# Attention heads taken in groups of 512 columns, with GpSimd subtracting the maxima of class heads, and differential attention in the tile order 3, 0, 2, 1

## Chip, cores and metric

One core of one Trainium2 chip. The metric is the device time of one launch in microseconds; of the kernel before three runs are shown.

## The reference, cut to what matters

The model has two blocks of two layers, all in float32, for 512 tokens of width 1024. The change touches four kinds of attention.

```python
# first block, in both layers: 8 plain heads over 2 key heads, width 64
sc = einsum('bqgrd,bkgd->bgrqk', qi, k) * scale
o = einsum('bgrqk,bkgd->bqgrd', softmax(sc), v)
# and three dilated groups of 4 heads: window 128 at step 1, 512 at 4, 2048 at 16
sc = where(valid, einsum('bqhd,bqkhd->bhqk', qi, kg) * scale + bias, -inf)
lse = logsumexp(sc); o = einsum('bhqk,bqkhd->bqhd', exp(sc - lse), vg)
# the three groups are merged by softmax over their lse
# second block, layer 0: differential attention, 8 heads, causal
p = softmax(where(dist >= 0, q @ k + bias, -inf))      # two maps m = 0, 1
attn = p[:, :, 0] - lam_full * p[:, :, 1]; out = attn @ v
# second block, layer 1: causal window of 128, 8 heads over 2 key heads, a sink a head
p = softmax(concatenate([q @ k + bias, sink]))[..., :-1]; out = p @ v
```

## The kernel before, in words

Tokens lie on the 128 partitions in NT = 4 tiles. The kernel is a chain of stages; `stage` (L63) ends each with a barrier of all engines. In a stage each engine runs its own program in order, and they meet at semaphores. `Link` (L50) makes DVE wait for its own last instruction.

**`attention` (L1564)** serves the first block's attention (called at L2362 from `first_layer`, once for each of the two layers, in a loop) and the window attention (called at L3580 from `odd_mixer`). Its work is a list of units, one unit being one head and one query tile. `global_units` (L2383) makes 32 units with 512 keys, `dilated_units` (L2394) 48: for each tile and head one "band" unit with 256 keys (step 1) and two "class" units with 128 keys (tokens are sorted by class, so that the wider steps become dense blocks of 128). `odd_mixer` makes 32 units of 256 keys, 128 in the first tile.

For unit i, PE multiplies queries and keys into one of four PSUM banks (L1610, 64 of the 128 rows; heads with even number lie on partitions 0 to 63, odd ones on 64 to 127). DVE finds the row maximum: L1658 for plain heads, negated in one step; with a bias L1665 adds it, writes the sum to `sc` and takes the maximum, and L1668 negates. In the window attention L1667 takes the sink into the maximum. ACT takes the exp with the negated maximum as its bias and the sum as its accumulator output (L1642; L1641 for the sink). PE transposes the result in blocks of 128 (L1617), DVE copies them out of PSUM (L1675), PE multiplies with V (L1627 through `chain`, L84) and DVE scales with the reciprocal of the sum, or, for dilated heads, only copies (L1682 to L1688). PE's order in step i is: scores of i+2, transposes of i-1, products of i-2; DVE's: maxima of i, copy of i-2, result of i-3. 12 warm-up products (`warm_up`, L98) stand at the start. SyncE meanwhile loads the bias tables, writes 11.8 MB of zeros to `slots_x` and brings V of the band heads into order through DRAM (`order_v0`, L1540); the first dilated unit waits for all of that.

`branches` (L1692) merges the dilated results on DVE (L1864 to L1887) beside PE's gates; `in_projection` (L1362) writes V.

**`diff_attention` (L3113)** has 32 units: 8 heads, in each the tiles t = 0, 1, 2, 3 with 128 (t + 1) keys. The two maps of a head lie on partitions 0 to 63 and 64 to 127. For each unit:

```python
link(V.tensor_tensor_reduce(sc.., ps.., b, 1.0, 2 * NEG, ALU.add, ALU.max, mx..))   # L3216, m = 0, 1
V.tensor_scalar(nm.., mx.., -1.0, None, ALU.mult)                                 # L3218
link(V.reciprocal(l, l)); link(V.tensor_tensor(l[:, 1:2], l[:, 1:2], nlam[:], ALU.mult))
link(V.tensor_scalar(p0, p0, l[:, 0:1], None, ALU.mult))                          # L3226
V.scalar_tensor_tensor(p0, p1, l[:, 1:2], p0, ALU.mult, ALU.add)                  # L3227
```

DVE runs the maxima of unit i, then combines the maps of unit i-1. ACT runs the exps of i (L3178), the copy of the transposes of i-1 (L3186) and the output copy of i-2 (L3191); half-way it rounds the next weights (`round_ahead`, L706).

## Time and profile before

| | |
|---|---|
| runs | 3630.17 us median of 3 (3629.97 to 3633.74) |
| the profiled execution's own time | 3633.27 us |
| its span in the profile | 3631.5 us |
| PE, PEld, DVE | busy 3201.4, 2543.0, 2324.2 us |
| ACT, POOL | busy 1214.5, 374.9 us |
| mean granted clock of PE | 0.919 |

PE is TensorE's matrix products, PEld its weight loads, DVE VectorE, ACT ScalarE, POOL GpSimd, SP SyncE. Matrix products are pipelined and their ends are modelled, so their durations overlap; starts are safer to subtract. The granted clock is a share of full speed. In a group, "idle before" is the time that the engine stood still ahead of those instructions, with what ended it.

### The profile page before, as it was taken

What the parts mean: (1) busy time and instruction counts of PE and PEld (TensorE: products, weight loads), DVE (VectorE), ACT (ScalarE), POOL (GpSimd) and SP (SyncE); (2) the same over time, 40 slices, a digit from 0 to 9 for tenths busy, and PEclk for the clock granted to TensorE, in tenths of its full rate; (3) what the DMA queues carried; (4) which work ended last, traced back from release to release, by engine and by line L of the source; (5) the groups of instructions that cost most, each with busy time, mean ns of one, the idle gap of its engine ahead of it and who ended that gap; (6) DMA issues with size and microseconds to landing.
All of it is one profiled execution on the core that took longest, in us unless ns stands there. A gap on an engine that the chain in (4) does not pass through costs nothing. (4 is left out here: it accounts for less than half of the span.)

```text
span 3631.5 us, 40689 instructions
## 1 busy us (share of the span) xinstructions
PE 3201.4 (88%) x14731; PEld 2543.0 (70%) x14731; DVE 2324.2 (64%) x3761; ACT 1214.5 (33%) x1713; POOL 374.9 (10%) x136
## 2 busy tenths in 40 slices
PE   4999996996799896899499789889999898989999
PEld 3777775774676685777377578757887687658887
DVE  6766666897676657599733747667664575564445
ACT  2323224664323322476322624431111222231111
POOL 0000001000000000100000000304444000004443
PEclk9999996998799998799789799989999899869999
DMA  7751724997655353599652034024442452103222
GB/s 256 238 171 61 242 101 141 360 405 278 216 171 168 135 185 99 193 401 403 243 170 100 1 102 139 27 82 133 148 144 74 136 182 79 53 24 105 92 92 81
DMA packets 285304, 583.89 MB, mean 161 GB/s; under 512 B 21561, under 2 KB 129537, under 8 KB 278076
## 3 DMA queue, kind: packets, MB, share of 16 engines
q1 hardware_dynamic: 272744, 537.83, 42.8%
q10 hardware_dynamic: 7764, 26.85, 1.8%
q0 software_dynamic: 4608, 16.78, 1.2%
q8 instruction: 109, 1.79, 0.2%
q14 instruction: 79, 0.65, 0.1%
HBM read 529.44 MB, written 78.70 MB: 167 GB/s over the span
## 5 line engine op out<-in xcount | busy, mean ns | idle before, releaser
L132 ACT CAST w_hi<-ring 128x2048 fp32r<-128x2048 f32 (+2 forms) x166 | 308.1, 1859 | 1213.5 <-PE ps L283 1030.9
L283 PE MATMUL ps<-hT_hi,w_hi 128*128 128x512 f32 (+1 forms) x1256 | 501.1, 399 | 25.2 <-DVEq L1117 12.6
L283 PE MATMUL ps<-hT_lo,w_hi 128*128 128x512 f32 (+1 forms) x1256 | 498.6, 397 | 0.0
L139 POOL TENSOR_TENSOR w_lo<-ring,w_hi 128x2048 fp32r<-128x2048 f32 x64 | 307.2, 4802 | 935.9 <-ACTq L2854 552.7
L144 DVE TENSOR_TENSOR w_lo<-ring,w_hi 128x2048 fp32r<-128x2048 f32 (+3 forms) x112 | 245.4, 2195 | 233.5 <-ACT w_hi L132 233.2
L283 PE MATMUL ps<-hT_hi,w_lo 128*128 128x512 f32 (+1 forms) x1256 | 305.2, 395 | 10.2 <-DVE w_lo L144 10.2
L283 PEld LDWEIGHTS ps<-hT_hi,w_hi 128*128 128x128 f32 (+1 forms) x1256 | 238.6, 190 | 85.6 <-DVEq L1117 14.2
L283 PEld LDWEIGHTS ps<-hT_hi,w_lo 128*128 128x128 f32 (+1 forms) x1256 | 235.7, 188 | 67.3 <-DVE w_lo L144 12.2
L1054 DVE SCALAR_TENSOR_TENSOR piece_sums<-pieces,cond,piece_sums 128x512 f32<-128x512 f32 x294 | 220.7, 751 | 90.4 <-DMA pieces<-in_w_ada_dram 57.8
L283 PEld LDWEIGHTS ps<-hT_lo,w_hi 128*128 128x128 f32 (+1 forms) x1256 | 238.6, 190 | 55.5
L283 PE MATMUL ps<-w_hi,hT_hi 128*128 128x512 f32 (+1 forms) x672 | 259.9, 389 | 1.0 <-ACT w_hi L132 1.0
L283 PE MATMUL ps<-w_hi,hT_lo 128*128 128x512 f32 (+1 forms) x672 | 259.0, 387 | 0.0
L283 PE MATMUL ps<-w_hi,hid_hi 128*128 128x512 f32 x448 | 174.4, 389 | 0.0
L283 PE MATMUL ps<-w_hi,hid_lo 128*128 128x512 f32 x448 | 174.4, 389 | 0.0
L2919 DVE TENSOR_TENSOR hid_exact<-hid_exact 128x512 f32<-128x512 f32 x64 | 162.0, 2531 | 4.0 <-DVE hid_exact L2916 0.6
L283 PE MATMUL ps<-w_lo,hT_hi 128*128 128x512 f32 (+1 forms) x672 | 158.2, 387 | 0.0
L2058 POOL DMA_INDIRECT slots_x<-ring,rows_r x16 | 21.5, 1345 | 1212.9 <-DVE rows_r L2271 1208.6
L283 PEld LDWEIGHTS ps<-w_hi,hT_hi 128*128 128x128 f32 x672 | 126.4, 188 | 28.6 <-issue 1.8
L283 PEld LDWEIGHTS ps<-w_hi,hT_lo 128*128 128x128 f32 x672 | 126.4, 188 | 26.8
L102 PE MATMUL ps<-ident_sb 128*128 128x128 f32 x664 | 99.7, 324 | 49.6 <-PEq L72 49.6
L283 PEld LDWEIGHTS ps<-w_lo,hT_hi 128*128 128x128 f32 x672 | 124.2, 188 | 27.3 <-DVE w_lo L144 0.3
L102 PEld LDWEIGHTS ps<-ident_sb 128*128 128x128 f32 x664 | 97.6, 238 | 52.9 <-issue 52.9
(594 smaller groups left out, 6258.3 us busy)
## 6 DMA issues: line engine op xcount, KB each, us to landing
ring<-in_mlp_w_dram SPq DMA_DIRECT2D x64, 1024.0 KB, 5.2
pieces<-in_w_ada_dram SPq DMA_DIRECT2D x96, 512.0 KB, 6.0
ring<-in_w_in_dram SPq DMA_DIRECT2D x36, 1024.0 KB, 7.0
pieces<-in_mod_w_dram SPq DMA_DIRECT2D x72, 512.0 KB, 5.3
raw_sep<-in_w_exp_gate_dram SPq DMA_DIRECT2D x50, 512.0 KB
raw_sep<-in_w_exp_up_dram SPq DMA_DIRECT2D x50, 512.0 KB
raw_sep<-in_w_exp_down_dram SPq DMA_DIRECT2D x24, 1024.0 KB
ring<-in_e_w_in_dram SPq DMA_DIRECT2D x24, 1024.0 KB, 5.5
```

What stands on the lines that cost most here:

```text
L102: pe.matmul(k.ps[:, bank, 0:P], k.ident[:], k.ident[:], start=True, stop=True)
L132: self.k.nc.scalar.copy(self.k.parts[0][:, i, 0:words], self.k.ring[:, i, 0:words]).then_inc(self.high, 1)
L139: self.k.nc.gpsimd.tensor_tensor(self.k.parts[1][:, i, 0:words], self.k.ring[:, i, 0:words], self.k.parts[0][:, i, 0:words].bitcast(F32), ...
L144: self.k.nc.vector.tensor_tensor(self.k.parts[1][:, i, 0:words], self.k.ring[:, i, 0:words], self.k.parts[0][:, i, 0:words].bitcast(F32), ...
L283: mm = pe.matmul(out, a if weight_left else b, b if weight_left else a, start=first and part == 0 and q == ks[0] and o == 0, stop=last and ...
L1054: ins = V.scalar_tensor_tensor(acc, slot[:, q, :], f, acc, ALU.mult, ALU.add)
L2058: nc.gpsimd.indirect_dma_start(k.slots_x, bass.IndirectOffsetOnAxis(rows[:, i, t:t + 1], 0), xn[:, t, :], None).then_inc(scattered, 16)
L2919: link(V.tensor_tensor(e, e, e, ALU.mult))
```

## The change

The units become groups that fill one PSUM bank of 512 columns: one plain head, four class heads, two band heads, and two window heads (four in the first tile). The two groups of a pair lie on opposite halves of the partitions, and PE takes their scores head by head in turn, for two groups ahead. For dilated and window groups one DVE instruction adds the bias and one takes all maxima, negated; for class groups GpSimd subtracts the maxima and ACT takes one exp of 512 columns. V of the dilated heads gets a 65th column of ones, so that the product brings the sum and the exp needs no accumulator. ACT makes the copies of the transposes for every second plain group and for all others. `sc` has three buffers for two, `pr` three for four. The window attention has 28 warm-up products. In the differential attention the maxima come out negated, the scale of p0 moves into the output copy, and the tiles go in the order 3, 0, 2, 1.

The diff, cut to its core (not shown: the layout of the bias tables, the `[:, :, 0:HD]` in the copies of `in_projection`, `order_v0` with 260-wide rows, the views in `branches`):

```diff
@@ in_projection
+            link(V.memset(T["vc"][:, :, :, HD:HD + 1], 1.0))
+            link(V.memset(v0c[:, :, :, HD:HD + 1], 1.0))
@@ attention(k, groups, loads=(), space=None, late=(), ahead=None, warm=12)
-        pr, sc, pT = idle[:, 0:4], idle[:, 4:6], idle[:, 6:8]
+        pr, sc, pT = idle[:, 0:3], idle[:, 3:6], idle[:, 6:8]
+        width = lambda i: 512 // heads(i)
+        of_class = [u["kind"] == "dilated" and len(u["heads"]) == 4 for u in groups]
+        by_act = [u["kind"] != "global" or i % 2 == 1 for i, u in enumerate(groups)]
@@ tensor
+            def scores(a):
+                b = a + 1
+                if b >= 4:
+                    pe.wait_ge(exp_done, b - 3)
+                for h in range(heads(a)):
+                    last_a, last_b = score(a, h), score(b, h)
+                last_a.then_inc(s_ready, 1)
+                last_b.then_inc(s_ready, 1)
+            warm_up(k, pe, 4, warm)
             for i in range(-2, N + 2):
+                if i % 2 == 0 and i + 2 < N:
+                    scores(i + 2)
                 if 1 <= i <= N:
...
-                    for j in range(W(v) // P):
+                    for j in range(4):
...
+                    for h, (_q, _k, vs) in enumerate(groups[v]["heads"]):
+                        n, w = vs[0].shape[-1], width(v)
+                        mm = chain(pe, k.ps[:, 4 + v % 2, h * n:(h + 1) * n], lambda j: pT[:, v % 2, h * w + j * P:h * w + (j + 1) * P],
+                                   lambda j: vs[j], range(len(vs)))
@@ scalar
+            def soften(i):
...
+                if u["kind"] == "global":
+                    last = nc.scalar.activation(p, k.ps[:, bank[i % 4], :], ACT.Exp, bias=nm(i), accum_out=ls[:, i % 4, 0:1])
+                elif of_class[i]:
+                    last = nc.scalar.activation(p, sc[:, i % 3], ACT.Exp)
+                else:
+                    w = width(i)
+                    if u["kind"] == "window":
+                        nc.scalar.activation(es[:, i % 4, 0:heads(i)], es[:, i % 4, 0:heads(i)], ACT.Exp)
+                    for h in range(heads(i)):
...
+                        last = nc.scalar.activation(p[:, at], sc[:, i % 3, at], ACT.Exp, bias=nm(i)[:, h:h + 1], accum_out=total)
+            for i in range(N + 1):
+                if i < N:
+                    soften(i)
+                v = i - 1
+                if v >= 0 and by_act[v]:
+                    act.wait_ge(t_ready, v + 1)
+                    if v >= 2:
+                        act.wait_ge(o_ready, v - 1)
+                    nc.scalar.copy(pT[:, v % 2], k.ps[:, 2 + v % 2, :]).then_inc(t_act, 1)
@@ gpsimd
+            for i in range(N):
+                if of_class[i]:
+                    pool.wait_ge(max_done, i + 1)
+                    x = per_head(sc[:, i % 3], i)
+                    nc.gpsimd.tensor_tensor(x, x, bcast(nm(i), 2, width(i)), ALU.add).then_inc(less_done, 1)
@@ vector
+            def maxima(i):
...
+                if u["kind"] == "global":
+                    V.tensor_reduce(nm(i), s, AX, ALU.max, negate=True).then_inc(max_done, 1)
+                    return
...
+                if i >= 3:
+                    dve.wait_ge(exp_done, i - 2)
+                x = per_head(sc[:, i % 3], i)
+                link(V.tensor_tensor(x, per_head(s, i), u["bias"], ALU.add))
+                ins = V.tensor_reduce(nm(i), x, AX, ALU.max, negate=True)
+                if u["kind"] == "window":
+                    link(ins)
+                    link(V.tensor_tensor(nm(i), nm(i), u["less_sink"], ALU.min))
+                    ins = V.tensor_tensor(es[:, i % 4, 0:heads(i)], nm(i), u["less_sink"], ALU.subtract)
+                ins.then_inc(max_done, 1)
...
+            for i in range(-1, N + 2):
+                if i + 1 < N:
+                    maxima(i + 1)
+                v = i - 1
+                if 0 <= v < N and not by_act[v]:
...
+                if i >= 2:
+                    result(i - 2)
@@ diff_attention
-        units = [(h, t) for h in range(8) for t in range(NT)]
+        units = [(h, t) for h in range(8) for t in (3, 0, 2, 1)]
@@ scalar
-                        last = nc.scalar.activation(pr[:, i % 2, m, 0:W(i)], sc[:, i % 2, m, 0:W(i)], ACT.Exp,
+                        last = nc.scalar.activation(pr[:, i % 2, m, 0:W(i)], sc[:, i % 2, m, 0:W(i)], ACT.Exp, scale=-1.0,
...
-                    nc.scalar.copy(y[:, t, h * P:(h + 1) * P], k.ps[:, 6 + u % 2, 0:P]).then_inc(o_out, 1)
+                    nc.scalar.activation(y[:, t, h * P:(h + 1) * P], k.ps[:, 6 + u % 2, 0:P], ACT.Copy, scale=inv[:, u % 4, 0:1]).then_inc(o_out, 1)
@@ vector
-                        link(V.tensor_tensor_reduce(sc[:, i % 2, m, 0:W(i)], k.ps[:, 2 * (i % 2) + m, 0:W(i)], b, 1.0, 2 * NEG,
-                                                    ALU.add, ALU.max, mx[:, i % 2, m:m + 1]))
-                    V.tensor_scalar(nm[:, i % 2, :], mx[:, i % 2, :], -1.0, None, ALU.mult).then_inc(max_done, 1)
+                        V.tensor_tensor_reduce(sc[:, i % 2, m, 0:W(i)], k.ps[:, 2 * (i % 2) + m, 0:W(i)], b, -1.0, -2 * NEG,
+                                               ALU.add, ALU.min, nm[:, i % 2, m:m + 1]).then_inc(max_done, 1)
...
+                    if u >= 4:
+                        dve.wait_ge(o_out, u - 3)
+                    link(V.reciprocal(inv[:, u % 4, :], l))
+                    link(V.scalar_tensor_tensor(r, l[:, 0:1], inv[:, u % 4, 1:2], nlam[:], ALU.mult, ALU.mult))
...
-                    link(V.tensor_scalar(p0, p0, l[:, 0:1], None, ALU.mult))
-                    V.scalar_tensor_tensor(p0, p1, l[:, 1:2], p0, ALU.mult, ALU.add).then_inc(p_ready, 1)
+                    V.scalar_tensor_tensor(p0, p1, r, p0, ALU.mult, ALU.add).then_inc(p_ready, 1)
@@ retention_projection
+                    link(V.tensor_scalar(sink[:], sink[:], -1.0, None, ALU.mult))
@@ odd_mixer
+            attention(k, groups, warm=28, space=space, late=moves, ahead=[(ring(i), wo[:, KD:KD + 4, 512 * i:512 * (i + 1)]) for i in range(2)])
```

## Rows read from the trace of the kernel before

**Rows 1.** Busy time by stage: us, busy us (xinstructions) by engine, clock, DMA, GB/s.
```profile
213.60:292.70 79.10, 79.04 (x445) 52.95 (x446) 53.04 (x120) 26.20 (x65) 0.00 (x0) 1.00 0.60 193
292.70:345.80 53.10, 52.23 (x316) 39.73 (x316) 44.09 (x249) 25.44 (x96) 0.00 (x0) 1.00 0.01 1
1987.00:2087.50 100.50, 74.83 (x382) 51.48 (x381) 74.17 (x297) 61.35 (x196) 0.00 (x0) 0.80 0.07 23
3131.00:3201.30 70.30, 66.70 (x257) 48.13 (x257) 49.22 (x257) 25.59 (x97) 0.00 (x0) 0.62 0.18 68
```

**Rows 2.** Timeline, plain heads: start us, us, engine, line, operation, tiles, count.
```profile
287.68 1.12 PE L1610 MATMUL ps<-kaT,qaT 64*128 64x512 f32 x2
...
288.73 0.66 PE L1617 MATMUL ps<-ident_sb,ring 128*128 128x128 f32 x4
...
289.12 0.97 PEld L84 LDWEIGHTS ps<-kva,ring 128*128 128x128 f32 x8
...
290.15 0.29 PEld L1610 LDWEIGHTS ps<-k0T,q0T 64*128 64x128 f32 x2
```

**Rows 3.** Timeline of PE, differential attention: both maps' scores of one tile.
```profile
1993.30 1.13 PE L3148 MATMUL ps<-kT,qT 64*128 64x512 f32 x4
...
2008.14 0.49 PE L3148 MATMUL ps<-kT,qT 64*128 64x128 f32 x4
```

**Rows 4.** Timeline of PE, dilated heads: two scores and the transposes after them.
```profile
335.71 0.49 PE L1610 MATMUL ps<-kcT,qcT 64*128 64x128 f32 x2
336.13 0.33 PE L1617 MATMUL ps<-ident_sb,ring 128*128 128x128 f32 x1
...
336.56 0.70 PE L1610 MATMUL ps<-k0T,q0T 64*128 64x256 f32 x2
337.19 0.44 PE L1617 MATMUL ps<-ident_sb,ring 128*128 128x128 f32 x2
```

**Rows 5.** Groups of instructions by shape, GpSimd: xcount, busy us, mean ns, idle before.
```profile
L2998 POOL TENSOR_TENSOR Xdec<-Xdt,dte 128x256 f32<-128x256 f32 x16 | 9.8, 612 | 536.7 <-DVE Xdt L3074 531.7 <-PE ps L3068 5.0
...
L3001 POOL TENSOR_TENSOR xh<-xh,par 128x1024 f32<-128x1024 f32 x4 | 7.8, 1946 | 0.0
```

**Rows 6.** Groups by shape, whole span, DVE and ACT.
```profile
L1642 ACT ACTIVATE ring<-ps,nm 128x512 f32<-128x512 f32 x64 | 44.0, 687 | 104.7 <-DVE nm L1658 104.4
...
L1658 DVE TENSOR_REDUCE nm<-ps 128x1 f32<-128x512 f32 x64 | 43.6, 682 | 10.8 <-PE ps L1610 10.8
...
L1642 ACT ACTIVATE ring<-ring,nm 128x128 f32<-128x128 f32 x64 | 25.7, 402 | 21.1 <-DVE nm L1668 20.8
...
L1675 DVE COPY ring<-ps 128x256 f32<-128x256 f32 x32 | 13.6, 425 | 10.0 <-PE ps L1617 9.8
```

**Rows 7.** Timeline of SyncE's queue in the attention of the first layer.
```profile
265.26 1.56 SPq L1594 DMA_DIRECT2D v<-scratch  x3
```

**Rows 8.** Timeline of PE, window attention: warm-up, then one unit.
```profile
3131.19 4.38 PE L102 MATMUL ps<-ident_sb 128*128 128x128 f32 x24 [3.54 <-PEq L72]
...
3153.45 1.22 PE L1610 MATMUL ps<-skT,sqT 64*128 64x256 f32 x2
3154.60 0.69 PE L1617 MATMUL ps<-ident_sb,attention_space 128*128 128x128 f32 x2
3155.08 0.95 PE L84 MATMUL ps<-skv,attention_space 128*128 128x64 f32 x4
3155.96 1.22 PE L1610 MATMUL ps<-skT,sqT 64*128 64x256 f32 x2
```

**Rows 9.** Timeline of DVE, differential attention: maxima at the start of two heads.
```profile
2010.33 0.28 DVE L3216 CUSTOM_DVE_ANT_0 attention_space<-ps,bias 128x128 f32<-128x128 f32 x1
...
2021.28 0.28 DVE L3216 CUSTOM_DVE_ANT_0 attention_space<-ps,bias 128x128 f32<-128x128 f32 x1
```

**Rows 10.** Groups by shape, differential attention: the scaling of p0, the output copy.
```profile
L3226 DVE TENSOR_SCALAR attention_space<-attention_space,dls 128x512 f32<-128x512 f32 x8 | 3.9, 486 | 0.3
...
L3191 ACT COPY y<-ps 128x128 f32<-128x128 f32 x32 | 8.6, 267 | 11.4 <-PE ps L84 11.2
```

More of the change, by code:

```diff
@@ L1561, in qkd_dst, with attention @@
     return dst, p, mul
-def attention(k, units, loads=(), space=None, late=(), ahead=None):
+def attention(k, groups, loads=(), space=None, late=(), ahead=None, warm=12):
     nc = k.nc
@@ new lines, in result @@
+            def result(v):
+                u, n = groups[v], heads(v)
+                dve.wait_ge(o_ready, v + 1)
+                d = u["heads"][0][2][0].shape[-1]
+                po = k.ps[:, 4 + v % 2, 0:n * d]
+                if u["kind"] == "dilated":
+                    V.tensor_copy(u["out"], po.rearrange("p (h d) -> p h d", h=n)).then_inc(o_out, 1)
+                    return
+                l = ls[:, v % 4, 0:n]
+                if u["kind"] == "window":
+                    link(V.tensor_tensor(l, l, es[:, v % 4, 0:n], ALU.add))
+                link(V.reciprocal(l, l))
+                if n == 1:
+                    V.tensor_scalar(u["out"], po, l, None, ALU.mult).then_inc(o_out, 1)
+                else:
+                    V.tensor_tensor(u["out"], po.rearrange("p (h d) -> p h d", h=n), bcast(l, 2, d), ALU.mult).then_inc(o_out, 1)
@@ L2380, in first_layer, with global_groups @@
                mod=(next_sums[:, 0:2 * D], A["b_ada"][DEPTH - 1][0:2 * D], 16, k.mod, (8,), None))
-def global_units(T):
-    units = []
-    for h in range(A_HEADS):
-        p0, g = 64 * (h % 2), h // 4
+def global_groups(T):
+    groups = []
+    for pair in range(A_HEADS // 2):
         for t in range(NT):
-            units.append(dict(q=T["qaT"][p0:p0 + 64, h // 2, t * P:(t + 1) * P], k=T["kaT"][p0:p0 + 64, g, :],
-                              v=[T["kva"][:, j, 128 + 64 * g:192 + 64 * g] for j in range(NT)],
-                              out=T["oa"][:, t, h * HD:(h + 1) * HD]))
-    return units
@@ new lines, in global_groups, with dilated_groups @@
+    return groups
+def dilated_groups(T, band, cls):
+    groups = []
+    for t in range(NT):
+        for odd in range(2):
+            rows, heads = slice(64 * odd, 64 * odd + 64), []
+            for g in range(2):
+                for half in range(2):
+                    q, kk = (T[n][rows, 2 * g + half, t * P:(t + 1) * P] for n in ("qcT", "kcT"))
+                    heads.append((q, kk, [T["vc"][:, t, BG * g + 2 * half + odd, :]]))
+            u = T["U12"][:, 2 * t + odd].rearrange("p g h d -> p (g h) d")
+            groups.append(dict(kind="dilated", heads=heads, bias=cls[:, odd], out=u[:, :, 0:HD + 1], nm=u[:, :, HD + 1]))
+        for odd in range(2):
+            rows, heads = slice(64 * odd, 64 * odd + 64), []
+            for half in range(2):
+                heads.append((T["q0T"][rows, half, t * P:(t + 1) * P], T["k0T"][rows, half, t * P:t * P + 256],
+                              [T["v0"][:, t + j, 2 * half + odd, :] for j in range(2)]))
+            u = T["U0"][:, 2 * t + odd]
+            groups.append(dict(kind="dilated", heads=heads, bias=band[:, 0 if t == 0 else 2 if t == NT - 1 else 1, odd],
+                               out=u[:, :, 0:HD + 1], nm=u[:, :, HD + 1]))
+    return groups
@@ L3579, in odd_mixer @@
             ring = lambda i: k.ring[:, i, :].rearrange("p (k n) -> p k n", k=4)
-            attention(k, units, space=space, late=moves, ahead=[(ring(i), wo[:, KD:KD + 4, 512 * i:512 * (i + 1)]) for i in range(2)])
+            attention(k, groups, warm=28, space=space, late=moves, ahead=[(ring(i), wo[:, KD:KD + 4, 512 * i:512 * (i + 1)]) for i in range(2)])
             hT = pair_of(nc, h, "hT", [P, KD, S], side="right")
```

226 lines of the change are left out of this document (100 added, 126 removed).

## The prediction

> **What bounds the kernel now.** I first took the busy table of four stretches [rows 1]: the plain heads of the first block's attention (214 to 293 us; the second layer repeats it at 1097), its dilated heads (293 to 346), the differential attention (1987 to 2087) and the window attention (3131 to 3201). The reader is to see that PE is busy for nearly the whole of the first two at a granted clock of 1.00, that no engine is full in the third (clock 0.80), and that the fourth has PE full at 0.62. The two layers' attention fills 265 us, the other two 166 us; the rest of the 3631 us is hardly touched.
>
> The timeline says what PE does there. One plain head and tile takes 2.47 us, from its score at 287.68 to the next at 290.15 [rows 2]: score 1.05 (to 288.73), four transposes 0.39 (to 289.12), eight products with V 1.03. PE is the bound. In the differential attention, where the two maps' scores lie in different halves of the array's rows, both 512-wide scores take 1.13 us and both 128-wide ones 0.49 [rows 3]; a single head's 128-wide score lasts as long, 0.49, and the next transpose starts 0.42 after it [rows 4]. So a pair in opposite halves costs what one costs. The change makes such pairs everywhere.
>
> **Plain heads (32 units a layer).** Heads 2k and 2k+1 go through the same tile as a pair. PE per pair: scores 1.06 (the 1.05 of rows 2, with 0.01 for the second as 1.13 stands to 1.12), transposes 2 x 0.39, products 2 x 1.03: 3.90, or 1.95 a unit against 2.47. Do the others keep up? DVE is busy 53.0 us for 32 units now [rows 1], 1.66 each, and gives every second copy (0.68, as the 512-wide maximum on PSUM in rows 6) to ACT: 1.32 of 1.95. ACT's 26.2 us are 0.82 each, with half a copy 1.17. I followed one pair round, PE's cycle from 0 to 3.9: its first products end at 2.5, DVE then moves that result, takes the next maximum (to 3.6), copies the transposes (to 4.4), moves the second result, takes the second maximum (to 5.5); ACT, behind its own copy (to 6.1), has the second exp by 7.0, and the scores that wait for it come at 7.8. So PE stays the bound, with 0.8 to spare: 32 x 0.52 = 16.6 us, less 1 for filling the pipeline, **-16 a layer**. From below it is 0 if pairs don't overlap; from above 16.6. The last loads that the dilated heads wait for start at 265.26 and are issued by 266.8 [rows 7]; the first dilated maximum moves from 292.7 to about 277, so 10 us of cover are left.
>
> **Dilated heads (48 units become 16 groups of 512 columns).** PE for two class groups: four pairs of 128-wide scores at 0.42 [rows 4], 1.68; transposes 0.78; products 2.06: 4.52. For two band groups: two pairs of 256 at 0.63, 1.26 + 0.78 + 2.06 = 4.10. Mean 2.16 a group. Now the loop through the others: DVE adds the bias and takes four maxima in one instruction; each is 512 wide, so each 0.68 as the plain maximum, 1.41 for both with gaps. It moves a result out in 0.43 [rows 6]. GpSimd's subtraction of 512 columns is not in the trace: 256 take 0.61 and 1024 with a broadcast 1.95 [rows 5], so about 1.05; at the least 0.61, at the most 1.95. Exp 0.69 at most. From the end of one group's products: result 0.43, maxima 1.41, result 0.43, maxima 1.41, GpSimd 1.05, exp 0.69, eight handovers of 0.05, then scores 1.68, transposes 0.39 and products 1.03 on PE: 8.9 us for four groups, 2.23 a group. So the chain of DVE and GpSimd binds by a hair, and PE waits 3%. The new waits in it: ACT's exp for GpSimd, with the copy of the group before queued behind it, and PE's paired scores for the exp of two pairs ago, with the next transposes behind them. 16 x 2.23 = 35.7, and 3 for the last group's tail: 38.7 against 53.0 now (292.7 to 345.7), **-14 a layer**. Bounds: GpSimd at 0.61 leaves PE as the bound (-15.5); at 1.95 four groups take 9.8 and it is -11.
>
> Here the Trainium skill speaks against the change. "GPSIMD Engine Reference", section 8, says that GpSimd shares its SBUF interfaces with DVE, and that DVE's instructions with two SBUF inputs or in a two-port mode get in its way. No row here shows the two side by side in such a stage; by that rule the subtraction moves towards the 1.95 bound.
>
> **Window attention (32 units become 14 groups).** The stage goes at two rates. From 3151.3 PE runs at half clock: scores of 256 take 1.15 (3153.45 to 3154.60), two transposes 0.48, four products 0.88 [rows 8]; a unit 2.51, two units 5.0. A new group, two heads, takes 1.15 (its pair's scores shared by two) + 0.96 + 1.76 = 3.87 there. At full clock a group's DVE work binds: 1.41 as above and six small ones. DVE's 49.2 us for 32 units [rows 1] are 1.54 each, of which two 256-wide ones take 0.85 and five small ones 0.69, so 0.14 each or 0.2 with gaps: 2.5 us to 2.6. I take 6 groups at 2.5 and 8 at 3.87, 46, and 4 for start and tail: 50 against 65.8 now (3135.5 to 3201.3). Before it stand 28 warm-up products for 12: those 24 instructions took 4.38 us [rows 8], 0.18 each, and at the higher clock at the least half of it: 32 more cost 2.9 to 5.8, I take 5. **-11**; bounds -2 (all at half, long warm-up) and -23 (all at full).
>
> **Differential attention (32 units).** A head of four units takes 10.95 us between its first maxima [rows 9]. DVE loses the negation of the maxima (some 0.08 of time a unit) and the scaling of p0, 0.49 for the widest and less in step for the others, 1.7 a head with gaps [rows 10]; the scale moves into ACT's copy of the output, where a pointer operand costs between nothing and 0.13 more on 0.27 (a whole 128-wide exp with its pointer takes 0.40) [rows 6, 10]. So 1.9 us of DVE work a head goes. It sits in a loop (maxima, exp, combine, transpose, copy) in which PE waits longest for DVE, so most of it counts: I take 1.6. The new order puts a 512-wide tile next to a 128-wide one, so that a long maxima stands beside a short combine; I give it nothing of its own, since the first head starts later by 0.8 and the last unit's tail is shorter by about 1. 8 x 1.6 = **-13**; bounds 0 and -23 (DVE without any idle time, 2.9 a head). The added wait for the output copy of unit u-4 holds up the combine on DVE and with it PE's transposes; that copy is three units old by then, so it is free.
>
> **Small edits.** Two memsets with a link at the start of the projection, while DVE waits for weights; copies to 65-wide rows of the same 512 columns; one more short add for the merged heads, beside PE's gates; one scaling of the sinks. +1 in all.
>
> **Sum:** -32 - 28 - 11 - 13 + 1 = -83. The profiled execution took 3633.3 us, so 3550; it stands 3.1 above the median of 3630.2, so **3548 us**.
>
> **Rivals.**
> (a) PE's clock falls in the dilated stage. For: the chain is as long as PE's own work, so PE waits a little in each group, and in the window stage, with PE busy 95%, the rows fall to half rate and stay there for 50 us [rows 1, 8]. Against: the dilated stage of before, in which DVE is as close to full, holds 1.00 to its tail. Price, from the half-rate rows: four groups take 3.1 and 2.3 for scores (1.15 stands to 0.63 as 1.83), 3.8 for transposes, 7.0 for products, so a group 4.07 against 2.23, 59 us over both layers: 3607. Chance 0.14.
> (b) The slower side: it falls in the plain stage too. A unit would take (1.93 + 1.92 + 3.52) / 2 = 3.7 against 1.95, 112 us more over both layers, 171 with the dilated: 3719; from half of both stages at half clock on, the kernel is slower than before. For: transposes become a larger share of PE's work. Against: PE has work in every microsecond there. Chance 0.05. The Trainium skill, "TensorE: Matmul & The Clock Gate", Part 4, says that transposes don't count as activity for the clock gate; by that rule this rival is likelier, but no row of before shows it, since the dilated stage with its transposes holds full clock.
> (c) The pairs don't overlap where heads change from product to product, since only two maps of one head are seen to. Plain heads +34 (32 pairs of 1.06), dilated +24 (2.94 for four groups), window +4: 3610. Chance 0.06.
> (d) It goes better: the window stage stays at full clock (-12), the differential attention loses nearly all its idle time (-10), GpSimd is quicker (-3): 3523. Chance 0.20.
> My forecast, 3530 to 3570, has 0.50; what lies in between the cases, 0.05.
>
> **Numbers.** The range reaches over (d) and most mixtures with (a): 3515 to 3600. 0.2% (7 us) is about what a measurement of this kernel can tell from no change. Faster 0.93, same 0.02, slower 0.05.
>
> **What would show it.** Right: a plain pair in 3.9 us, with two 512-wide scores in 1.1; dilated groups at 2.2 to 2.3 with GpSimd's instruction near 1.05 us; a head of the differential attention at 9.3; window groups at 2.5, then 3.9. Wrong: scores of a pair one after the other; a granted clock of 0.5 between 217 and 320 us; GpSimd over 1.5 us; PE waiting for DVE in the plain stage; a head that stays near 11 us.

## The result

The changed kernel takes 3510.86 us (median of 4 runs, 3501.62 to 3512.78), the kernel before 3630.42 us beside it: ratio 0.9664, 95% interval 0.9646 to 0.9682, or 120 us less. The prediction had 3548 us and 3515 to 3600: the direction was right, the gain was half as large again as forecast, and the median lies 4 us below the range.

| | before | after |
|---|---|---|
| the profiled execution's own time, us | 3633.27 | 3511.61 |
| its span, us | 3631.5 | 3509.8 |
| PE, PEld, DVE busy, us | 3201.4, 2543.0, 2324.2 | 3075.4, 2487.9, 2230.2 |
| ACT, POOL busy, us | 1214.5, 374.9 | 1220.9, 391.8 |
| mean granted clock of PE | 0.919 | 0.932 |

To find where 122 us of span went, I cut both traces at the same marks: a stage runs from the first DVE or ACT instruction of its function to the first one of the next function. These cuts are used for every experiment below.

| stage, us | before | after | difference | forecast |
|---|---|---|---|---|
| attention, first layer | 133.3 | 97.9 | -35.4 | -30 |
| attention, second layer | 133.3 | 97.9 | -35.4 | -30 |
| differential attention | 139.1 | 120.9 | -18.3 | -13 |
| window attention | 72.0 | 52.3 | -19.7 | -11 |
| projection behind the window | 64.9 | 56.7 | -8.2 | 0 |
| the scan behind the differential attention (`ssd`) | 156.5 | 149.4 | -7.1 | 0 |
| all others, with the MLP behind the scan at +3.7 | | | +2.4 | +1 |

The four stretches of [rows 1] in the kernel after. Columns: start and end in us, its length, busy us (and instructions) of PE, PEld, DVE, ACT and POOL, the granted clock, the share of the DMA engines and GB/s.

```profile
214.30:276.40 62.10, 61.31 (x463) 48.00 (x463) 39.87 (x106) 33.36 (x80) 0.00 (x0) 1.00 0.74 246
276.40:311.00 34.60, 33.35 (x300) 30.14 (x299) 27.43 (x56) 20.14 (x42) 8.38 (x8) 1.00 0.01 1
1911.00:1996.00 85.00, 65.47 (x392) 44.41 (x392) 58.57 (x233) 63.65 (x199) 0.00 (x0) 0.92 0.09 27
3037.00:3087.50 50.50, 40.08 (x289) 35.79 (x289) 30.69 (x99) 25.80 (x93) 0.00 (x0) 0.84 0.25 95
```

PE still fills the first two, at a clock of 1.00. In the other two no engine is full, and the clock rose: 0.80 to 0.92 and 0.62 to 0.84. The plain heads, from the timeline of PE (start, us, engine, line, operation, tiles, count):

```profile
262.05 1.13 PE L1618 MATMUL ps<-kaT,qaT 64*128 64x512 f32 x4
263.11 0.66 PE L1641 MATMUL ps<-ident_sb,ring 128*128 128x128 f32 x4
263.60 1.00 PE L84 MATMUL ps<-kva,ring 128*128 128x64 f32 x8
264.44 0.61 PE L1641 MATMUL ps<-ident_sb,ring 128*128 128x128 f32 x4
264.88 1.00 PE L84 MATMUL ps<-kva,ring 128*128 128x64 f32 x8
265.81 1.13 PE L1618 MATMUL ps<-kaT,qaT 64*128 64x512 f32 x4
```

Both 512-wide scores of a pair take 1.06 us start to start, where the single one of [rows 2] took 1.05, and a pair takes 3.76 us in place of two units of 2.47. One turn of the dilated heads, all engines, with the weight loads left out:

```profile
289.80 1.16 PE L1618 MATMUL ps<-kcT,qcT 64*128 64x128 f32 x16
...
290.90 0.66 PE L1641 MATMUL ps<-ident_sb,ring 128*128 128x128 f32 x4
...
291.39 1.00 PE L84 MATMUL ps<-vc,ring 128*128 128x65 f32 x8
...
292.43 0.43 DVE L1733 COPY U<-ps 128x260 f32<-128x260 f32 x1 [0.97 <-PE ps L84]
...
292.78 0.68 DVE L1719 TENSOR_TENSOR ring<-ps,cls 128x512 f32<-128x512 f32 x1
...
293.50 0.69 DVE L1720 TENSOR_REDUCE U<-ring 128x4 f32<-128x512 f32 x1
293.61 0.73 PEld L1618 LDWEIGHTS ps<-k0T,q0T 64*128 64x128 f32 x8
293.61 1.13 PE L1618 MATMUL ps<-k0T,q0T 64*128 64x256 f32 x8
294.10 0.42 DVE L1733 COPY U<-ps 128x260 f32<-128x260 f32 x1
294.27 1.05 POOL L1699 TENSOR_TENSOR ring<-ring,U 128x512 f32<-128x512 f32 x1 [5.18 <-DVE U L1720]
294.44 0.68 DVE L1719 TENSOR_TENSOR ring<-ps,cls 128x512 f32<-128x512 f32 x1
...
295.92 1.05 POOL L1699 TENSOR_TENSOR ring<-ring,U 128x512 f32<-128x512 f32 x1 [0.61 <-DVE U L1720]
...
297.00 0.63 ACT L1672 ACTIVATE ring<-ring 128x512 f32<-128x512 f32 x1 [0.55 <-POOL ring L1699]
...
297.69 1.16 PE L1618 MATMUL ps<-kcT,qcT 64*128 64x128 f32 x16
```

Read it as the loop of the prediction: the products with V end at 292.4, DVE moves a result, adds the bias and takes the maxima, moves the next result, does it again for the second group, then GpSimd takes its 1.05 us (from 295.92) and ACT its exp (from 297.00), whose end PE's scores at 297.69 follow. The next scores of k0T come 7.88 us after those at 285.73. The differential attention, from DVE's timeline, the first maxima of two heads (a head now begins with its widest tile):

```profile
1936.60 0.69 DVE L3293 CUSTOM_DVE_ANT_0 attention_space<-ps,bias 128x512 f32<-128x512 f32 x1 [0.36 <-PE ps L3225]
...
1944.97 0.69 DVE L3293 CUSTOM_DVE_ANT_0 attention_space<-ps,bias 128x512 f32<-128x512 f32 x1 [0.36 <-PE ps L3225]
```

A head takes 8.37 us, where [rows 9] had 10.95. And the window attention, two groups at full clock, next to [rows 8] at half clock:

```profile
3058.07 1.14 PE L1618 MATMUL ps<-skT,sqT 64*128 64x256 f32 x8
3059.14 0.66 PE L1641 MATMUL ps<-ident_sb,attention_space 128*128 128x128 f32 x4
3059.64 1.00 PE L84 MATMUL ps<-skv,attention_space 128*128 128x64 f32 x8
3060.48 0.60 PE L1641 MATMUL ps<-ident_sb,attention_space 128*128 128x128 f32 x4
3060.92 1.00 PE L84 MATMUL ps<-skv,attention_space 128*128 128x64 f32 x8
3062.62 1.13 PE L1618 MATMUL ps<-skT,sqT 64*128 64x256 f32 x8 [0.70 <-ACT attention_space L1680]
```

### The profile page after: what moved, and what is told of

Same layout as the page of the kernel before. It is cut to its first block and busy times, and to the rows that moved or that the text cites. A ratio compares the mean times of both kernels' runs of the same rounds, so it can differ in the third digit from the quotient of the medians.

```text
span 3509.8 us, 39676 instructions
## 1 busy us (share of the span) xinstructions
PE 3075.4 (88%) x14763; PEld 2487.9 (71%) x14763; DVE 2230.2 (64%) x3130; ACT 1220.9 (35%) x1629; POOL 391.8 (11%) x152
## 5 line engine op out<-in xcount | busy, mean ns | idle before, releaser
L3015 DVE TENSOR_TENSOR y<-y,ps 128x512 f32<-128x512 f32 x48 | 33.0, 688 | 157.1 <-PE ps L283 155.8
```

The lines of the kernel that those rows point to most:

```text
L3015: link(V.tensor_tensor(yv, yv, k.ps[:, 4 * b + t, :], ALU.add))
```

## The experiments

| run | us (median) | ratio to before, 95% interval |
|---|---|---|
| p1_first_block | 3561.25 | 0.9808 (0.9777 to 0.9840) |
| p2_differential | 3616.43 | 0.9949 (0.9933 to 0.9965) |
| p3_window | 3610.04 | 0.9942 (0.9925 to 0.9959) |
| p4_warm_up_alone | 3632.15 | 0.9995 (0.9981 to 1.0010) |
| q1_order_undone | 3508.95 | 0.9665 (0.9645 to 0.9685) |
| q2_order_alone | 3628.18 | 0.9983 (0.9970 to 0.9996) |
| q3_short_warm_up | 3517.59 | 0.9691 (0.9670 to 0.9711) |
| q4_subtraction_on_DVE | 3515.44 | 0.9676 (0.9653 to 0.9699) |
| r1_GpSimd_twice | 3531.27 | 0.9722 (0.9695 to 0.9749) |
| r2_unpaired_scores | 3580.27 | 0.9861 (0.9835 to 0.9887) |
| r3_round_on_GpSimd | 3511.07 | 0.9671 (0.9646 to 0.9695) |
| r4_scaling_back_on_DVE | 3521.24 | 0.9692 (0.9658 to 0.9725) |
| s1_window_unpaired | 3528.16 | one run |
| s2_window_order_1230 | 3510.56 | 0.9663 (0.9639 to 0.9687) |
| s3_all_three | 3506.23 | 0.9644 (0.9625 to 0.9663) |

On the chips of these runs the kernel before ranged from 3621 to 3643 us, wider than in the first comparison; differences of a few us are therefore read from the stages of the profiled executions, not from the medians.

### The parts, each alone

**p1_first_block**: the new attention for the two layers of the first block; the differential and window attention as before.

```diff
-def diff_attention(...):   # after
+def diff_attention(...):   # before
-            attention(k, groups, warm=28, space=space, ...)
+            unit_attention(k, units, space=space, ...)
```

> The new groups in the attention of the first block's two layers alone; the differential and the window attention as before. Theory: all of the gain that the trace shows in these two stages is their own: 133.3 us become 97.9 each, so -71, and the 3.7 us between the two layers belong to them too (the merging of the heads): 3555 us. Rival: what lies outside the touched stages (-12 us in all) is a change of the granted clock that comes with any shift in time; then the stages give -71 as well, but the rest moves by several us either way, and stages that are not touched here show another clock than in the kernel before.

The two stages took 99.5 and 99.4 us, the kernel 70.5 us less: the gain of these stages is their own. The 1.6 us over the 97.9 of the changed kernel is a stretch of 3.4 us at half clock that the records show in the first 5 us of the stage, in its warm-up: those 24 instructions took 4.55 us here and 2.92 in the first layer of the changed kernel. It comes in some executions of either kernel and not in others (134.9 against 133.3 in the kernel before). Two other stages differ with the same code: `ssd` took 156.3 us here and the projection behind the window 64.9, where the changed kernel has 149.4 and 56.7.

**p2_differential**: the new `diff_attention` in the kernel before.

```diff
-def diff_attention(...):   # before
+def diff_attention(...):   # after
```

> The new differential attention alone, the rest as before. Theory: a head takes 8.4 us in place of 10.95 whatever stands ahead of it, the stage gives -19: 3611 us. Rival: part of those 19 us came from the granted clock, which was 0.92 in this stage after the change and 0.80 before, because the stage began at another time; then heads take 9 us or more here, and the kernel 3616 or more.

A head took 8.37 us, exactly as in the changed kernel, although the stage began 73 us later; the stage took 117.7 us against 139.1. So the gain doesn't hang on when the stage begins, and the rival's usual heads of 9 us or more didn't come. The kernel's median, 3616, is the rival's all the same: in the profile `ssd` and the projection behind the window stand at 157.6 and 65.2 us. How much of the head's gain comes through the clock is seen below.

**p3_window**: the groups and 28 warm-up products in the window attention of the kernel before.

```diff
-            attention(k, units, space=space, ...)
+            group_attention(k, groups, warm=28, space=space, ...)
```

> The new groups and the long warm-up in the window attention alone, the rest as before. Theory: groups keep the array busy enough for the full clock, 2.3 us a group, the stage gives -20, and the projection after it starts at full clock and gives some 7 more: about 3604 us. Rival: it was luck of the clock; then groups at half clock take 3.9 us, the stage gives -11 or less and nothing follows: 3619 us or more.

The stage took 54.4 us and the projection behind it 62.6, where the changed kernel has 52.3 and 56.7. The stage's gain comes with the groups and their pairs (s1 parts the two); what follows it varies (below).

**p4_warm_up_alone**: 28 warm-up products for 12 in the window attention of the kernel before.

```diff
-            attention(k, units, space=space, ...)
+            attention(k, units, warm=28, space=space, ...)
```

> The kernel before with 28 warm-up products in place of 12 in the window attention, its 32 single units unchanged. Theory: the warm-up only costs, 3 to 5 us, and the units fall to half clock as before: 3633 to 3635 us. Rival: the longer warm-up is what lifts the clock; then a unit of 2.5 us takes about 1.5 for most of the stage, and the kernel is 10 to 20 us faster.

The stage took 77.0 us, against 72.0 to 75.0 in the profiles with 12 products and single units, and from 20 us after its start to its end, 57 us, its records show half clock (52 in the kernel before). The warm-up alone brings nothing and costs 2 to 5 us.

The three parts sum to -70.5 - 15.3 - 21.7 = -107.5 us, the whole is -119.6. The touched stages alone, in the profiles, gave 67.8 + 21.5 + 17.6 = 106.9 us one by one and 108.8 together. So the difference of 12 us lies in stages that none of them touches: `ssd` takes 149.2 to 157.6 us over the profiles of the study and the projection behind the window 56.7 to 65.2, each with one and the same code, by how many stretches at half clock fall into them. In the profile of before both stood near their long end (156.5, 64.9), in that of after near their short one.

### The scores of a pair

**r2_unpaired_scores**: each group's scores by themselves.

```diff
-                if i % 2 == 0 and i + 2 < N:
+                if i + 2 < N:
                     scores(i + 2)
...
-                b = a + 1
-                if b >= 4:
-                    pe.wait_ge(exp_done, b - 3)
+                if a >= 4:
+                    pe.wait_ge(exp_done, a - 3)
                 for h in range(heads(a)):
-                    last_a, last_b = score(a, h), score(b, h)
-                last_a.then_inc(s_ready, 1)
-                last_b.then_inc(s_ready, 1)
+                    last = score(a, h)
+                last.then_inc(s_ready, 1)
```

> The changed kernel with each group's scores issued by themselves, as before the change, one group ahead of the other; everything else stays grouped. Leaves the pairs of opposite halves out. Theory: the pairs are the gain of the plain heads and a good part of that of the dilated ones. A plain unit is 2.4 us again, +16 us a layer; two class groups' scores take 3.4 in place of 1.16 and two band groups' 2.5 in place of 1.13, so +3.6 for four groups or +14 a layer; the window +8: about 3580 us in all. Rival: grouping and the split of the copies between DVE and ACT are the gain, PE had been waiting more than its records say; then less than +10 a layer.

A layer's attention took 123.9 us (+26), the window stage 72.9 (+20.6), the kernel 3580 us, as expected in sum but not in its terms. PE's timeline, plain heads first, then the dilated ones:

```profile
249.70 1.12 PE L1618 MATMUL ps<-kaT,qaT 64*128 64x512 f32 x2
250.75 0.66 PE L1639 MATMUL ps<-ident_sb,ring 128*128 128x128 f32 x4
251.25 1.00 PE L84 MATMUL ps<-kva,ring 128*128 128x64 f32 x8
252.18 1.12 PE L1618 MATMUL ps<-kaT,qaT 64*128 64x512 f32 x2
...
301.88 1.16 PE L1618 MATMUL ps<-kcT,qcT 64*128 64x128 f32 x8
302.97 0.66 PE L1639 MATMUL ps<-ident_sb,ring 128*128 128x128 f32 x4
...
304.40 1.13 PE L1618 MATMUL ps<-k0T,q0T 64*128 64x256 f32 x4
305.45 0.66 PE L1639 MATMUL ps<-ident_sb,ring 128*128 128x128 f32 x4
```

A plain unit is back at 2.48 us, 1.2 more a pair; from the first maximum to the dilated heads' a layer took 74.6 us for 58.0. But four class scores of one group, one after the other, take 1.09 us, so 0.27 each, where I had put 1.7, and two band scores 1.05, where I had put 1.25. The 0.42 of [rows 4] is a score that stands alone in front of a transpose; in a run of scores it costs less. Four dilated groups took 10.0 us for 7.88, +2.1 and not +3.6, and the window stage made up for it with +20.6 where I had +8.

### What sets the dilated stage

**q4_subtraction_on_DVE**: DVE subtracts the maxima.

```diff
                 ins = V.tensor_reduce(nm(i), x, AX, ALU.max, negate=True)
+                if of_class[i]:
+                    link(ins)
+                    V.tensor_tensor(x, x, bcast(nm(i), 2, width(i)), ALU.add).then_inc(less_done, 1)
+                    return
```

> The changed kernel with the subtraction of the class heads' maxima on DVE in place of GpSimd. Theory: the chain through DVE and GpSimd sets the dilated stage (7.88 us for four groups); it loses two handovers and one 1.05 and gains 0.7 twice, and it delays the result behind it, so 8.2 to 8.6 us, +2 to +3 us a layer. Rival 1: PE sets it, with the chain just under it; then DVE, at 5.6 us of 7.9 now and 7.0 then, still hides, and nothing changes within 1 us. Rival 2: GpSimd's instruction holds up DVE through their shared interfaces; then DVE's own instructions get shorter and the stage is faster than 97.9 us a layer.

Four groups took 8.21 us and a layer 101.5; of its +3.6, 1.6 is the half clock in the warm-up again, and the dilated part took 37.8 us for 35.8. The loop sets the stage, as expected; PE, with 33.35 of 34.6 us busy, comes just under it. The rival of shared interfaces falls: DVE's additions of the bias take 0.68 us here, without GpSimd, as they do beside it.

**r1_GpSimd_twice**: the subtraction is made twice.

```diff
+                    if sum(of_class[:i]):
+                        pool.wait_ge(spare_done, sum(of_class[:i]))
...
+                    nc.gpsimd.tensor_tensor(twice..., x, bcast(nm(i), 2, width(i)), ALU.add).then_inc(spare_done, 1)
                     nc.gpsimd.tensor_tensor(x, x, bcast(nm(i), 2, width(i)), ALU.add).then_inc(less_done, 1)
```

> The changed kernel with GpSimd's subtraction made twice (the first into a spare tile), 16 instructions of 1.05 us more over both layers, nothing else added. Theory: the loop of DVE, GpSimd, ACT and PE sets the dilated stage. Of two neighbouring class groups the second's instruction ends 1.5 us later (0.45 because the first's doubled one runs into it, 1.05 of its own), so four groups take 9.4 in place of 7.9 us: +6 us a layer. Rival: PE's own work sets it; then most of the 1.5 is hidden and a layer gains less than 3 us. If GpSimd also slowed DVE through shared interfaces, the 0.68 us additions of DVE beside it would get longer than they are.

The second layer took 104.5 us (+6.6; its turns 9.6, 10.8 and 9.2 us), as the loop says, the first 111.6 (+13.7, of which 1.6 in the warm-up). Columns as in the table of stretches, dilated heads of the first layer and the end of the second's attention:

```profile
278.00:325.00 47.00, 42.42 (x297) 38.27 (x296) 27.87 (x55) 20.55 (x41) 16.34 (x16) 0.78 0.01 1
1120.00:1160.00 40.00, 35.79 (x305) 31.16 (x305) 27.61 (x60) 19.40 (x42) 12.23 (x12) 0.96 0.04 13
```

With PE waiting 1.3 us or more in each turn (9.2 less 7.9) its clock fell for 20.5 us in the first layer and for 3.4 in the second. So my rival (a), a clock that falls in the dilated stage, didn't happen in any profile with one subtraction, and did with two. DVE's additions stood at 0.68 us again.

### The differential attention

**q1_order_undone** and **q2_order_alone**: the order of the tiles, in the changed kernel and in the one before.

```diff
-        units = [(h, t) for h in range(8) for t in (3, 0, 2, 1)]   # q1; q2 is the reverse
+        units = [(h, t) for h in range(8) for t in range(NT)]
```

> The changed kernel with the differential attention's query tiles in the order 0, 1, 2, 3 again. Theory of the prediction: the order is worth nothing, the gain is DVE's work that was left out; the stage from its start to the projection behind it stays at 121 us, within 2. Rival: the order is worth a good part, since a wide tile's long maxima no longer stand beside a narrow one's short exp; then the stage takes 126 us or more.

> The kernel before, with the order 3, 0, 2, 1 alone. Theory: nothing, the stage stays at 139 us within 2. Rival: it falls to 134 or less, and then the order and the removed instructions share the gain.

**r4_scaling_back_on_DVE**: the scaling of p0 as before, the order and the maxima as after.

```diff
+                    link(V.tensor_scalar(p0, p0, l[:, 0:1], None, ALU.mult))
-                        nc.scalar.activation(y[...], k.ps[...], ACT.Copy, scale=inv[:, u % 4, 0:1]).then_inc(o_out, 1)
+                        nc.scalar.copy(y[...], k.ps[...]).then_inc(o_out, 1)
```

> The changed kernel with the first map's weights scaled by DVE again and ACT's output copy without the scale; the left-out negation and the order stay. The prediction's own price: 1.7 us a head, nearly all of it on the path, 13 us in all: the stage takes 133 to 135 us. Rival: PE's and ACT's work is what is left there, with DVE busy 79%; then it costs 6 us or less, and the rest of the 18 us that the stage gained is from elsewhere (clock, order).

The usual distance between two heads' first maxima, at full clock but for the first row:

| us a head | order 0, 1, 2, 3 | order 3, 0, 2, 1 |
|---|---|---|
| DVE's work as before, with 3.4 to 3.8 us of each head at half clock | 10.85 (before) | |
| DVE's work as before | 10.04 (p1) | 9.76 (q2) |
| negation left out, scaling kept | | 8.96 (r4) |
| both left out | 8.59 (q1) | 8.37 (after) |

In the kernel before every head holds half clock. The 10.04 is in p1's profile, which has the old code here and two heads with 0.4 us of half clock or none; one of them, and beside it the head of [rows 9], in the columns of the stretches:

```profile
1924.09 0.28 DVE L3421 CUSTOM_DVE_ANT_0 attention_space<-ps,bias 128x128 f32<-128x128 f32 x1
...
1934.13 0.28 DVE L3421 CUSTOM_DVE_ANT_0 attention_space<-ps,bias 128x128 f32<-128x128 f32 x1
```

```profile
1924.10:1934.10 10.00, 7.09 (x46) 4.65 (x46) 9.00 (x37) 7.06 (x25) 0.00 (x0) 1.00 0.01 2
```

```profile
2010.30:2021.30 11.00, 8.56 (x46) 5.76 (x46) 9.17 (x38) 7.19 (x25) 0.00 (x0) 0.84 0.00 0
```

At full clock the order is worth 0.3 us a head with DVE's old work and 0.2 with the new, and the left-out work 1.45 in the old order and 1.4 in the new: they add up, to 1.7. The other 0.8 of the 2.5 us is half clock, which the usual heads lose with either edit. Over the whole stage the records show 51 us of it before, 38 with the order alone (q2), 27 with the left-out work alone (q1) and 24 after. The stage took 135.1 us in q2 (139.1 before, 138.7 to 141.2 in the other profiles with the old code), between the two cases of its expectation, and 121.1 in q1 (120.9), as the prediction had it. There the 0.2 us a head, 1.8 in all, is lost among other half-clock stretches and another first and last head; the kernel took 3509.

With the scaling kept (r4) the stage took 125.3 us, +4.4 and not the 13 of the prediction's price: 0.6 us a head. The rest of the 1.4, 0.8 (9.76 less 8.96), comes with the negation and the links around it, which stood between the maxima and the exp. Which of the two, instruction or links, was not tried.

**r3_round_on_GpSimd**: the two casts of the next projection's weights go from ACT's row to GpSimd.

```diff
-                if i == N // 2:
-                    round_ahead(k, act, ahead)
+        @block.gpsimd
+        def _(pool):
+            for i in range(2):
+                pool.wait_ge(k.ahead[i], ahead)
+                nc.gpsimd.tensor_copy(k.parts[0][:, i, :], k.ring[:, i, :])
```

> The changed kernel with the rounding of the weights of the next projection, two casts of 2048 columns, 3.7 us together, that stand in ACT's row halfway through the differential attention, given to GpSimd, which is idle there. Theory: the head that holds them takes 13.2 us where others take 8.4, so the stage falls from 121 by 4.5 to 5 us and the kernel to about 3506. Rival 1: GpSimd's casts slow DVE, which is busy 79% there, and half of it comes back. Rival 2: the half clock takes it back (granted 0.92 in this stage).

The fifth head fell from 13.2 to 8.37 us and the stage from 120.9 to 114.8, yet the kernel took 3511 as before: the window stage and its projection took 54.6 and 65.2 in place of 52.3 and 56.7, in code that isn't touched, with 27 and 38 us at half clock in place of 18 and 16. So rival 2 is right in its effect, but not in the stage that it named. GpSimd makes the casts in the first head, as soon as the weights have landed, and not halfway. DVE's and GpSimd's timeline shows one thing more:

```profile
1916.21 2.10 POOL L3275 CAST w_hi<-ring 128x2048 fp32r<-128x2048 f32 x1 [216.97 <-DMA ring<-in_e_w_out_dram]
...
1917.63 0.70 DVE L3306 SCALAR_TENSOR_TENSOR dratio<-dls,dinv,nlam 128x1 f32<-128x1 f32 x1
...
1918.88 1.90 POOL L3275 CAST w_hi<-ring 128x2048 fp32r<-128x2048 f32 x1 [0.56 <-DMA ring<-in_e_w_out_dram]
...
1919.37 0.16 DVE L3305 RECIPROCAL dinv<-dls 128x2 f32<-128x2 f32 x1
...
1919.57 1.22 DVE L3306 SCALAR_TENSOR_TENSOR dratio<-dls,dinv,nlam 128x1 f32<-128x1 f32 x1
1920.82 0.62 DVE L3308 SCALAR_TENSOR_TENSOR attention_space<-attention_space,dratio 128x384 f32<-128x384 f32 x1
```

### The window attention

**q3_short_warm_up**: 12 warm-up products in the changed kernel.

```diff
-            attention(k, groups, warm=28, space=space, ...)
+            attention(k, groups, space=space, ...)
```

> The changed kernel with 12 warm-up products in the window attention in place of 28. Theory: the 32 instructions less save 3 to 5 us and nothing else changes, groups stay at 2.3 us: the stage takes 48 us in place of 52. Rival: the warm-up is what brought the full clock; then groups start at 3.9 us and the stage takes 58 us or more.

51.0 us for the stage, of which its records show 14 at half clock in its middle (6.8 in the changed kernel): groups came to 2.3 us all the same. The warm-up is not what brings the full clock. The kernel took 3517.6 us, more than with 28 products, since the projection behind the window took 65.2 us for 56.7.

**s1_window_unpaired**: the scores as in r2, in this stage alone.

```diff
-                if i % 2 == 0 and i + 2 < N:
+                if i + 2 < N and groups[0]["kind"] == "window":
+                    single(i + 2)
+                elif i % 2 == 0 and i + 2 < N:
                     scores(i + 2)
```

> The changed kernel with the scores issued group by group in the window attention alone; its groups, its long warm-up and the pairs of the first block stay. Theory: it is the pairs that bring the window stage back to full clock, since all profiles with pairs show half clock for 7 to 14 us in it and all without (the single units, and the groups without pairs) for 55 to 65: the stage takes 72 to 75 us in place of 52. Rival: in the kernel without any pairs it stayed at half clock because the stage began at an unlucky time; then it comes back here and the stage takes about 58 us (six pairs of 1.1).

The stage took 72.9 us. Its row, and that of a whole stage of single units in the kernel before:

```profile
3033.00:3106.00 73.00, 68.57 (x297) 58.29 (x298) 31.78 (x100) 27.64 (x95) 0.00 (x0) 0.57 0.17 66
```

```profile
3131.20:3203.10 71.90, 68.50 (x265) 49.89 (x266) 49.41 (x258) 27.31 (x98) 0.00 (x0) 0.62 0.18 67
```

Without pairs the groups and the long warm-up together give this stage nothing (it took 72 to 75 us before); the pairs give all of it. In the ten profiles with pairs the clock falls 10 to 14 us after the stage's start and is back 3.4 to 13.7 us later; in the seven without it falls 13 to 20 us after the start and stays at half to the stage's end, 52 to 62 us, though PE has fewer gaps there (68.6 of 73 us busy against 40.1 of 50.5). In both the first 3 us of the stage are at half clock, and with pairs the last 8 to 11 too. The edit does two things: scores in opposite halves no longer alternate, and PE no longer issues two groups' scores in one go. Which of them brings the clock back, and why, is not shown; that the pairs as a whole do is.

**s2_window_order_1230**: the two groups of four heads last.

```diff
-            for t in range(NT):
+            for t in (1, 2, 3, 0):
```

> The changed kernel with the window attention's query tiles in the order 1, 2, 3, 0, so that the two groups of four heads, in which PE waits 2.8 and 1.1 us for ACT's eight exps, come last. Theory: the half clock that the records show 24.7 us after the stage's start in every profile comes from these waits at its start; it doesn't come, and the stage takes 46 to 49 us in place of 52 to 54. Rival: it comes all the same, since in a stage whose PE waits for ACT in each group it only takes time; then 52 us or more, and the tail is longer by the two slow groups.

53.7 us, and half clock comes 13.4 us after the stage's start again, for 10.2 us. (The expectation put it at 24.7 us, wrongly: in all eight profiles with pairs and 28 products the records have it 13.4 to 13.6 us after the start, and PE's timeline agrees, in which the same scores take 2.0 us there and 1.1 later.) The waits of those two groups are not its cause, and this theory falls.

**s3_all_three**: r3, s2 and q3 in one.

```diff
-            attention(k, groups, warm=28, space=space, ...)
+            attention(k, groups, space=space, ...)   # with the edits of r3 and s2
```

> The changed kernel with the weights' rounding on GpSimd in the differential attention, the window's query tiles in the order 1, 2, 3, 0 and 12 warm-up products there. If each gives what it should, -6 in the differential stage, -4 in the window's and -4 by the warm-up: 3498 us. Rival: the granted clock outside these stages moves by as much the other way, as it did in the run with the rounding alone: 3506 to 3511 us.

3506 us, ratio 0.9644. The window stage took 48.0 us and the differential 117.7, and the projection behind the window 65.2, at its long end. The interval overlaps that of the changed kernel (0.9646 to 0.9682), and the two did not run side by side: a gain of a few us is likely but not shown.

## Why the prediction was wrong

**Direction, mechanism, rivals.** Pairs of scores in opposite halves of the rows cost what one costs, in all three places: right, and rival (c) is out. The clock held in the plain and the dilated stage, so (a) and (b) are out. For rival (b) I had drawn on the Trainium skill ("TensorE: Matmul & The Clock Gate", Part 4), which says that transposes don't count as activity for the clock gate. The trace doesn't bear the rival out: the granted clock was 1.00 over both stretches of the first layer. Of (d) the window stage's full clock came for most of the stage. GpSimd was not quicker, and in the differential attention DVE kept its idle time, 26 us of the stretch before and after (100.50 less 74.17, 85.00 less 58.57).

**Plain heads, -16 a layer:** measured -17 (75.1 to 58.0 us from first maximum to the dilated heads'), a pair 3.76 us for 3.90. Right.

**Dilated heads, -14:** measured -18.4 (53.0 to 34.6). The loop was the right one and GpSimd's 1.05 us was right to the hundredth (1.041 to 1.051), but four groups took 7.88 us, not 8.9. The step that failed is the price of the class heads' scores, "four pairs of 128-wide scores at 0.42 [rows 4], 1.68": they took 1.10, because a score in a run of scores costs 0.27 us. That is 0.6 of the missing 1.0; the other 0.4 are the eight handovers of 0.05, which I added to durations that hold them already (DVE's starts are 0.72 apart for an instruction of 0.68). The same wrong price of a score made PE's own work, and with it my upper bound of -15.5, too small a gain. The subtraction did not move towards 1.95 us either. The Trainium skill ("GPSIMD Engine Reference", section 8) speaks of DVE's instructions with two SBUF inputs or in a two-port mode. Here DVE's additions read one input from PSUM and one from SBUF and its maxima a single one: GpSimd kept its 1.05 us beside them and the additions their 0.68, so the case with two SBUF inputs doesn't occur in this stage, and the rule stays untested here.

**Differential attention, -13:** measured -18.3 over the stage. A usual head fell by 2.5 us, not 1.6. The step that failed is the clock, which has no term here: the 10.95 of [rows 9] was taken as the head's price, and it holds 3.4 us at half clock that the new code doesn't have. At full clock a head went from 10.04 to 8.37, 1.7 us, and that the forecast's 1.6 comes so close is in part luck, for its parts were wrong: "I give it nothing of its own" for the order (0.3), 0.08 for the negation (0.8 with its links) and 1.7 for the scaling (0.6). The pointer scale in ACT's copy cost 0.10 (0.37 for 0.27), within its bounds, and the wait for an old output copy was free.

**Window attention, -11:** measured -19.7. Groups take 2.3 us at full clock, for 2.5, but the step that failed is "6 groups at 2.5 and 8 at 3.87": I carried the half clock of before over to the new groups, and with pairs it lasts 14 us or less in the middle of the stage (6.8 in the profile of after), beside some 3 at the start and 8 in the tail. Two groups at half clock took 7.1 us (q3), 3.55 each for 3.87. The warm-up cost 1.3 to 5.8 us (q3, p4, s2 against s3) for my 5.

**Outside, +1:** measured -13, of which -8.2 in the projection behind the window and -7.1 in the scan. No term stood for this. The stages of untouched code vary by 8 us each with the half-clock stretches that they catch, so of the 39 us between my -83 and the profile's -122, about 25 are sizes of terms (109 for 84) and 14 are this. With the terms right, the sum would have been -108, or 3522 us.

**The range** reached over (d), and (d) had the window and the differential gains together, but it had nothing for what lies outside the stages, and the upper bounds of the dilated stage were drawn from the same 0.42 as the forecast.

## What to carry to other kernels

Where a matmul uses half of the array's rows, put two that use different halves next to each other: here that took the second of each pair off PE's time (74.6 to 58.0 us for a layer's plain heads), and the window stage came back to full clock with it, which it did not by grouping alone. Price an instruction from a row where it stands as it will stand, in a run of its own kind or alone in front of another kind: here that was 0.27 against 0.42 us. And compare the parts of a gain only at the same granted clock: between the usual heads the order seems to give 1.1 us alone, the left-out work 2.3 and both 2.5, as if they covered the same stall. At full clock they add up (0.3 and 1.4 are 1.7), and the 0.8 that either takes away is half clock.

## What was not expected of the hardware

A DVE instruction of one column with three SBUF operands, 0.22 us elsewhere, took 0.70 and 1.22 us while GpSimd's casts of 2048 columns ran, and ended with the cast both times (1918.3 and 1920.8); maxima that read PSUM and SBUF in the same microseconds kept their 0.42 to 0.55. This agrees with the Trainium skill ("GPSIMD Engine Reference", section 8), which names DVE instructions with two SBUF inputs as those that contend with GpSimd. It cost little here: the head with both casts took 9.38 us, the same head in p2's profile 9.27. GpSimd's casts took 1.90 and 2.10 us, ACT's 1.89 each.

In the window stage without pairs (s1) PE, busy 57.3 of 59.4 us, stayed at half clock for all of them; with pairs (the changed kernel) it was back at full clock after 6.8 us, of which it was busy 5.7. The fuller PE was not the one with the higher clock.
